# Inner norms: all squares added on VectorE, sums and spread inside running units, and a branch product moved ahead

## The chip, the core and the metric

The kernel runs on one core of one Trainium2 chip. The metric is the device time of one execution in microseconds (us). The engines are TensorE (PE, its weight loads PEld), VectorE (DVE), ScalarE (ACT), GpSimd (POOL) and SyncE (SP), whose queue issues most DMAs.

## The reference

One sequence of 512 tokens of width 1024 goes through two blocks. Cut to what matters:

```python
h = h + 0.5 * swiglu(rmsnorm(h, ffn1_norm), ...)           # "ffn1"
u = rmsnorm(h, mix_norm)                                   # "mix"
(fq, fk, fv, ff, dq, dk, dv, iq, ik, iw, mq, g) = jnp.split(u @ w_in, SPLIT_POINTS, axis=-1)
...                                                        # three attentions o_a, o_b, o_c
proj = jnp.einsum('bsnw,nwd->bsnd', branches, w_branch)    # the branches
h = h + jnp.sum(sigmoid(g) * proj, axis=2) @ w_out
h = h + 0.5 * swiglu(rmsnorm(h, ffn2_norm), ...)           # "ffn2"
# second block
z = rmsnorm_2(h, g_mix_2) @ w_in_2 + b_in_2                # "mix2"
h = h + y @ w_out_2                                        # y: a convolution and a pooling of z
h = h + swiglu_2(rmsnorm_2(h, g_ffn_2), ...)               # "ffn3"
return rmsnorm_2(h, g_final)                               # "final"
```

`rmsnorm` divides each token by the root of the mean of its squares and multiplies by a gain. All is float32.

## The kernel before

Everything is held transposed: channels on 128 partitions, the 512 tokens along the free axis, so the residual `h` is 8 chunks of 128x512. Weights come as units of 128x1024, `RING` = 4 of them in flight. For exactness each factor is split in a rounded high part and a low rest, and `products` (L498 on) makes three matmuls of one step: high x high, weight low x high, weight high x low. A unit of a projection (`project`) is 8 such steps, 24 matmuls. For a unit, SyncE's queue loads the raw weight once the unit four earlier is done, ScalarE casts it to its high part (`high`, L984; called through `after(u)`, which casts unit u + 2), GpSimd subtracts to get the low part (`low_part`, L435), and TensorE waits for `low_done`.

A norm works like this. The product before it ends in eight banks. `feed` on VectorE adds each bank to the residual (L1411) and, one chunk later, makes the low part of the input (L1361); `feed` on ScalarE makes the input's high part (L992) and the square of the chunk (L995) into `tiles[m]`. The norm's factor is applied only behind the products, so TensorE starts at once with the first two units, interleaved (`pair_start`). The squares are added up: tiles 0 to 4 by GpSimd (`add_squares`, L451), tiles 5 to 7 and the total by VectorE (`total_squares`, L1378). `sums` on TensorE (L573) sums over channels, ScalarE takes the root (`feed_root`, L1006), VectorE the reciprocal (L1368), `spread_factor` on TensorE (L581) spreads it over the partitions, and VectorE copies it to `token_factor` (L1401), where every consumer of the products waits for it. At the first norm, ffn1, VectorE adds all squares, and sums and spread stand inside the third and the fourth unit. At the inner norms (mix, ffn2, mix2, ffn3) `sums` stands behind `pair_start` and `spread_factor` right behind it, ahead of the third unit.

In the gated layers VectorE scales the gate and the up product (L1426, L1431), ScalarE applies Silu (L1107), VectorE multiplies (L1436), ScalarE casts the hidden chunk (L1112), VectorE makes its low part (L1441). In ScalarE's program order the cast of the fifth unit's weights stands behind the first hidden chunk's cast.

In the mix projections each head norm squares its output, GpSimd makes the squares' low part (L480) and TensorE sums them (L655).

The branches: for chunk m = 0 to 7 of the output there are three products `branch(m, n)` of four steps each (12 matmuls); three products use one and a half weight units. Products (0, 0) and (0, 1) read attention outputs that are split early, (0, 2) those of the memory attention, which ScalarE casts (L1240) and VectorE splits (L1650, `out_split`) last. GpSimd then alternates weight products with the scaling of the last gates (L486).

Engines run their own instruction lists in program order and meet only through semaphores, so the order written in the code is the order on the engine.

## Time and profile before

| | us |
|---|---|
| median of 3 runs | 1805.9 |
| lowest, highest | 1804.47, 1806.55 |
| the profiled execution | 1804.1 |
| its span, first to last instruction | 1802.3 |
| TensorE matmuls busy | 1769.3 |
| VectorE, ScalarE, GpSimd busy | 696.1, 698.4, 798.7 |
| TensorE's mean granted clock | 0.997 of full speed |

A row of the timeline gives the start and the duration of an instruction, or of a few equal ones in a row (x8), and in brackets how long its engine idled before it and what ended that. Matmuls overlap: one of 512 columns is shown with 0.39 us, but the next starts after some 0.23 us, so lost time is best read from starts.

### The profile page before, as it was taken

The numbers are of one execution on the slowest core, as the hardware profiler recorded it, in microseconds if no ns is written. First come the engines' busy times: TensorE is split into PE (matmuls) and PEld (weight loads), VectorE is DVE, ScalarE is ACT, GpSimd is POOL, SyncE is SP. The second block draws the span as 40 slices with busy tenths as digits, with TensorE's granted clock in tenths as the row PEclk, the third lists the DMA queues.
The fourth block names the chain that finished last, engine by engine and source line by source line (L and its number), as shares of the span: only waits on it lengthen the run. The fifth ranks groups of instructions, "written<-read, shape, count | busy, mean of one in ns | idle before, by whom it ended". The sixth has DMA issues, their size and how long they took to land.

```text
span 1802.3 us, 23345 instructions
## 1 busy us (share of the span) xinstructions
PE 1769.3 (98%) x8472; PEld 1435.3 (80%) x8472; DVE 696.1 (39%) x1141; ACT 698.4 (39%) x1120; POOL 798.7 (44%) x368
## 2 busy tenths in 40 slices
PE   9999999999999999999999999999999999999997
PEld 7888888877887777787878888888766788888886
DVE  5222230077867875235252222200775422222002
ACT  5322321164544477784342232211425432322212
POOL 2444444456565433334444444444533444444442
PEclk9999999999999999999999999999999999999998
DMA  5222322322333121112222233223251222232231
GB/s 177 100 93 94 103 95 93 127 84 79 106 116 110 63 70 45 48 48 93 94 93 94 93 96 102 93 93 104 89 141 61 91 93 93 98 100 93 95 103 70
DMA packets 50495, 168.23 MB, mean 93 GB/s; under 512 B 6264, under 2 KB 7032, under 8 KB 50304
## 3 DMA queue, kind: packets, MB, share of 16 engines
q1 hardware_dynamic: 47088, 161.34, 27.3%
q10 hardware_dynamic: 3344, 6.05, 1.1%
q8 instruction: 40, 0.66, 0.2%
q14 instruction: 23, 0.19, 0.0%
HBM read 161.84 MB, written 2.11 MB: 91 GB/s over the span
## 4 chain that ended last, share of the span: by engine, by line
PE 91%; DVE 5%; ACT 2%; DMA 1%; issue 1%; SPq 0%; POOL 0%; DVEq 0%; ACTq 0%
PE bank L502 25%; PE bank L504 25%; PE bank L503 25%; PE bank L716 8%; PE bank L761 2%; DVE input_low L1361 2%; PE bank L787 2%; PE bank L884 1%; PE bank L778 1%; DMA raw_weights<-weights 1%; DVE bank L1511 1%; DVE residual L1411 1%; PE bank L581 0%; PE bank L767 0%; ACT tile L1193 0%
## 5 line engine op out<-in xcount | busy, mean ns | idle before, releaser
L435 POOL TENSOR_TENSOR weights_low<-raw_weights,weights_high 128x1024 fp32r<-128x1024 f32 x292 | 707.8, 2426 | 941.4 <-ACT weights_high L984 919.4
L502 PE MATMUL bank<-input_high,weights_high 128*128 128x512 f32 x1424 | 557.9, 392 | 6.1 <-DVE input_low L1361 5.3
L503 PE MATMUL bank<-input_high,weights_low 128*128 128x512 f32 x1424 | 554.4, 389 | 0.0
L504 PE MATMUL bank<-input_low,weights_high 128*128 128x512 f32 x1424 | 554.3, 389 | 0.0
L984 ACT CAST weights_high<-raw_weights 128x1024 fp32r<-128x1024 f32 x294 | 307.0, 1047 | 307.3 <-DMA raw_weights<-weights 290.0
L502 PEld LDWEIGHTS bank<-input_high,weights_high 128*128 128x128 f32 x1424 | 267.3, 188 | 69.2 <-DVE input_low L1361 8.8
L504 PEld LDWEIGHTS bank<-input_low,weights_high 128*128 128x128 f32 x1424 | 267.3, 188 | 56.2
L503 PEld LDWEIGHTS bank<-input_high,weights_low 128*128 128x128 f32 x1424 | 267.4, 188 | 54.4 <-issue 0.2
L502 PE MATMUL bank<-hidden_high,weights_high 128*128 (+1 forms) x528 | 205.4, 389 | 0.0
L503 PE MATMUL bank<-hidden_high,weights_low 128*128 (+1 forms) x528 | 205.4, 389 | 0.0
L504 PE MATMUL bank<-hidden_low,weights_high 128*128 (+1 forms) x528 | 205.4, 389 | 0.0
L1431 DVE TENSOR_TENSOR tile<-bank,token_factor 128x512 f32<-128x512 f32 x66 | 45.6, 691 | 300.3 <-PE bank L504 300.3
L1112 ACT CAST hidden_high<-tile 128x512 f32 (+1 forms) x66 | 41.1, 622 | 303.4 <-DVE tile L1436 303.4
L1411 DVE SCALAR_TENSOR_TENSOR residual<-bank,residual 128x512 f32<-128x512 f32 x40 | 27.3, 684 | 259.1 <-PE bank L504 259.1
L503 PEld LDWEIGHTS bank<-hidden_high,weights_low 128*128 128x128 f32 x528 | 99.1, 188 | 20.7
L502 PEld LDWEIGHTS bank<-hidden_high,weights_high 128*128 128x128 f32 x528 | 99.1, 188 | 20.5
L504 PEld LDWEIGHTS bank<-hidden_low,weights_high 128*128 128x128 f32 x528 | 99.1, 188 | 20.5
L1107 ACT ACTIVATE tile<-tile 128x512 f32<-128x512 f32 x66 | 41.9, 634 | 181.1 <-DVE tile L1426 181.1
L1426 DVE TENSOR_TENSOR tile<-bank,token_factor 128x512 f32<-128x512 f32 x66 | 45.7, 692 | 137.1 <-PE bank L504 136.2
L716 PE MATMUL bank<-input_high,weights_high 128*128 128x512 f32 x192 | 78.1, 407 | 0.4 <-DVE tile L1459 0.4
L716 PE MATMUL bank<-input_high,weights_low 128*128 128x512 f32 x192 | 76.8, 400 | 0.0
L716 PE MATMUL bank<-input_low,weights_high 128*128 128x512 f32 x192 | 76.7, 399 | 0.0
(243 smaller groups left out, 1844.2 us busy)
## 6 DMA issues: line engine op xcount, KB each, us to landing
raw_weights<-weights SPq DMA_DIRECT2D x294, 512.0 KB, 3.4
out_t<-out_t SPq DMA_DIRECT2D x8, 256.0 KB, 2.1
residual<-x_t SPq DMA_DIRECT2D x6, 256.0 KB, 5.8
glu_stacked<-glu_padded ACTq DMA_DIRECT2D x24, 64.0 KB, 3.8
glu_stacked<-glu_padded SPq DMA_DIRECT2D x24, 64.0 KB, 3.7
mem_in<-mem_t ACTq DMA_DIRECT2D x1, 1024.0 KB, 4.9
tile<-forget_sums ACTq DMA_DIRECT2D x4, 256.0 KB, 3.6
raw_weights<-weights SPq DMA_DIRECT2D x3, 256.0 KB, 5.6
```

Of the source, the lines that this page charges most:

```text
L435: pool.tensor_tensor(wl[:, u % RING, :], raw[:, u % RING, :], wh[:, u % RING, :].bitcast(F32), ALU.subtract).then_inc(low_done, 1)
L502: pe.matmul(out, wh[:, u % RING, w], rh, start=start, stop=False)
L503: pe.matmul(out, wl[:, u % RING, w], rh, start=False, stop=False)
L504: return pe.matmul(out, wh[:, u % RING, w], rl, start=False, stop=stop)
L716: mm = pe.matmul(bank[g % 2][:, :], (wl if part == 1 else wh)[:, u % RING, w], (xl if part == 2 else xh)[:, k, :], start=(k == 0 and part ...
L761: mm = pe.matmul(score_banks[n % 3][:, cols], left, right[:, cols], start=True, stop=not (kind == "fox" and last))
L984: act.copy(wh[:, u % RING, :], raw[:, u % RING, :]).then_inc(high_done, 1)
L1107: act.activation(tiles[c][:, :], tiles[c][:, :], ACT.Silu).then_inc(sem(f"{name}_silu"), 1)
L1112: act.copy(hh[:, f, :].rearrange("p a n -> p (a n)"), tiles[2 + c][:, :]).then_inc(sem(f"{name}_high"), 1)
L1411: dve.scalar_tensor_tensor(out=h[:, m, :], in0=bank[m][:, :], scalar=share, in1=h[:, m, :], op0=ALU.mult, op1=ALU.add).then_inc(sem("resid ...
L1426: dve.tensor_tensor(tiles[c][:, :], bank[2 * c][:, :], rstd[:, :], ALU.mult).then_inc(sem(f"{name}_gate"), 1)
L1431: dve.tensor_tensor(tiles[2 + c][:, :], bank[2 * c + 1][:, :], rstd[:, :], ALU.mult).then_inc(sem(f"{name}_banks"), 1)
```

## The change

Six things are changed.

1. At the inner norms VectorE adds all eight squares in one row of seven additions, as at ffn1; GpSimd adds none, but for the final norm.
2. In ffn2 and ffn3 the sums stand inside the third unit, behind its fourth step, and the spread inside the fourth unit, behind its second step. In mix and mix2 the sums stand behind the first step of the third unit and the spread behind its fourth.
3. In ffn2 and ffn3 ScalarE casts the fourth unit's weights ahead of the root.
4. In mix VectorE's two small casts of the ones (L1581, L1582) stand ahead of the additions.
5. The branches of chunks 0 and 1 come in the order (0,0), (0,1), (1,0), (0,2), (1,1), (1,2). GpSimd makes the low part of weight U_BR+2 ahead of the last gate's scaling, but only once all twelve outputs are split.
6. The sigmoids of chunk m wait for the gates of that chunk, not for all 24.

```diff
@@ gpsimd
             low_parts(DVE_LOWS, U_IN + 2)
-            add_squares("mix")
@@
                 low_part(gate_unit(g) + 2)
+                if g == GATES - 1:
+                    pool.wait_ge(sem("out_split"), 12)
+                    low_part(U_BR + 2)
                 pool.wait_ge(sem("gates_out"), g + 1)
                 pool.tensor_tensor(gate_slot(g), gate_slot(g), rstd[:, :], ALU.mult)
-            low_parts(U_BR + 2, U_GU2 + 2)
-            add_squares("ffn2")
+            low_parts(U_BR + 3, U_GU2 + 2)
             low_parts(U_GU2 + 2, U_IN2 + 2)
-            add_squares("mix2")
             low_parts(U_IN2 + 2, U_GU3 + 2)
-            add_squares("ffn3")
@@ tensor, project
                     if k == behind:
                         inside()
+                    if then and k == behind + 3:
+                        then()
@@ tensor, gate_up
-                    spread_factor(feed)
-                    project(u0 + 2, bank[2][:, :], xh, xl, u0 + 3)
-                    project(u0 + 3, bank[3][:, :], xh, xl, u0 + 4)
+                    project(u0 + 2, bank[2][:, :], xh, xl, u0 + 3, inside=lambda: sums(feed), behind=3)
+                    project(u0 + 3, bank[3][:, :], xh, xl, u0 + 4, inside=lambda: spread_factor(feed), behind=1)
@@ tensor, mix (and the same in mix2)
                         if j == 2:
-                            spread_factor("mix")
+                            project(U_IN + j, proj[j % 3][:, 0:n], rh, rl, U_IN + j + 1, n, inside=lambda: sums("mix"),
+                                    behind=0, then=lambda: spread_factor("mix"))
@@ tensor, branches
-            for m in range(DK):
+            for m, n in ((0, 1), (1, 0), (0, 2), (1, 1), (1, 2)):
+                branch(m, n)
+            for m in range(2, DK):
                 for n in range(3):
-                    if m or n:
-                        branch(m, n)
+                    branch(m, n)
@@ scalar, gate_up
                         if c == 0 and i is None:
-                            feed_root(feed_name, bank[4])
                             if u0:
                                 after(u0 + 1)
+                            feed_root(feed_name, bank[4])
@@ scalar, sigmoids
+                act.wait_ge(sem("gates_scaled"), 2 * DK + m + 1)
@@ vector, total_squares
-                for i, m in enumerate((*range(POOL_SQUARES + 1, DK), 0)):
...
+                for m in range(1, DK):
+                    dve.wait_ge(sem("input_square"), fed(name, m))
...
                     dve.tensor_tensor(tiles[0][:, :], tiles[0][:, :], tiles[m][:, :], ALU.add
                                       ).then_inc(sem("squares_totalled"), 1)
@@ vector, mix
             feed("mix", "mix_norm", "g1", U_IN - 1, 0.5)
+            dve.tensor_copy(bd_r[:, :], bd[:, :]).then_inc(sem("ones_rounded"), 1)
+            dve.tensor_copy(ones_r[:, :], ones[:, :]).then_inc(sem("ones_rounded"), 1)
             factor("mix")
             dve.wait_ge(sem("sine_signed"), P // HD)
-            dve.tensor_copy(bd_r[:, :], bd[:, :]).then_inc(sem("ones_rounded"), 1)
-            dve.tensor_copy(ones_r[:, :], ones[:, :]).then_inc(sem("ones_rounded"), 1)
```

How this reads on the engines. TensorE's list at the norm of mix, before; L573 are the sums, L581 the spread:

```order
L503 MATMUL bank<-input_high,weights_low 128x512
L504 MATMUL bank<-input_low,weights_high 128x512
L573 MATMUL bank<-ones,tile_107 128x1 x4
L581 MATMUL bank<-identity,token_root 128x128 x4
L502 MATMUL bank<-input_high,weights_high 128x512
L503 MATMUL bank<-input_high,weights_low 128x512
L504 MATMUL bank<-input_low,weights_high 128x512
```

and now, where the rows ahead of L573 belong to the third unit's first step:

```order
L504 MATMUL bank<-input_low,weights_high 128x512
L573 MATMUL bank<-ones,tile_107 128x1 x4
L502 MATMUL bank<-input_high,weights_high 128x512
L503 MATMUL bank<-input_high,weights_low 128x512
L504 MATMUL bank<-input_low,weights_high 128x512
L502 MATMUL bank<-input_high,weights_high 128x512
L503 MATMUL bank<-input_high,weights_low 128x512
L504 MATMUL bank<-input_low,weights_high 128x512
L502 MATMUL bank<-input_high,weights_high 128x512
L503 MATMUL bank<-input_high,weights_low 128x512
L504 MATMUL bank<-input_low,weights_high 128x512
L581 MATMUL bank<-identity,token_root 128x128 x4
```

The sums moved behind three matmuls, the spread behind nine more. ScalarE's list at ffn2, from the end of the feed, before; L984 casts a unit's weights, L1006 is the root, L1107 Silu, L1112 the cast of a hidden chunk:

```order
L995 ACTIVATE tile_114<-residual 128x512
L984 CAST weights_high<-raw_weights 128x1024
L1006 ACT_TABLE_LOAD
L1006 ACTIVATE token_root<-bank,epsilons 128x4
L984 CAST weights_high<-raw_weights 128x1024
L1107 ACT_TABLE_LOAD
L1107 ACTIVATE tile_107<-tile_107 128x512
L1112 CAST hidden_high<-tile_109 128x512
L984 CAST weights_high<-raw_weights 128x1024
L1107 ACTIVATE tile_108<-tile_108 128x512
```

and now, with the lines shifted by four:

```order
L999 ACTIVATE tile_114<-residual 128x512
L988 CAST weights_high<-raw_weights 128x1024 x2
L1010 ACT_TABLE_LOAD
L1010 ACTIVATE token_root<-bank,epsilons 128x4
L1111 ACT_TABLE_LOAD
L1111 ACTIVATE tile_107<-tile_107 128x512
L1116 CAST hidden_high<-tile_109 128x512
L988 CAST weights_high<-raw_weights 128x1024
L1111 ACTIVATE tile_108<-tile_108 128x512
```

The cast of the fourth unit's weights moved ahead of the root; that of the fifth still stands behind the first hidden chunk. GpSimd's list at the last gates, with the semaphores waited for, before:

```order
L486 TENSOR_TENSOR gates_last<-gates_last,token_factor 128x512 [waits gates_out]
L435 TENSOR_TENSOR weights_low<-raw_weights,weights_high 128x1024 [waits high_done]
L486 TENSOR_TENSOR gates_last<-gates_last,token_factor 128x512 [waits gates_out]
L435 TENSOR_TENSOR weights_low<-raw_weights,weights_high 128x1024 [waits high_done]
L486 TENSOR_TENSOR gates_end<-gates_end,token_factor 128x512 [waits gates_out]
L435 TENSOR_TENSOR weights_low<-raw_weights,weights_high 128x1024 [waits high_done] x2
```

and now:

```order
L489 TENSOR_TENSOR gates_last<-gates_last,token_factor 128x512 [waits gates_out]
L435 TENSOR_TENSOR weights_low<-raw_weights,weights_high 128x1024 [waits high_done]
L435 TENSOR_TENSOR weights_low<-raw_weights,weights_high 128x1024 [waits high_done,out_split]
L489 TENSOR_TENSOR gates_end<-gates_end,token_factor 128x512 [waits gates_out]
L435 TENSOR_TENSOR weights_low<-raw_weights,weights_high 128x1024 [waits high_done]
L442 UNCONDITIONAL_BRANCH
```

One weight product moved ahead of the last gate's scaling, with a wait of its own for the split outputs.

## Rows read from the trace of the kernel before

**Rows 1.** The page's part 1: busy us of each engine, its share of the span, instructions

```profile
PE 1769.3 (98%) x8472; PEld 1435.3 (80%) x8472; DVE 696.1 (39%) x1141; ACT 698.4 (39%) x1120; POOL 798.7 (44%) x368
```

**Rows 2.** Waits of TensorE, whole span: who, for whom, us in total, times, longest

```profile
PE bank L502 <- DVE input_low L1361: 5.3, 11, 0.8
PE bank L502 <- DVE mem_out_low L1650: 3.5, 3, 1.8
PE bank L581 <- DVE token_root L1368: 3.3, 5, 0.7
```

**Rows 3.** Timeline, TensorE, second norm (ffn2): start us, us, engine, line, operation, shapes, [idle]

```profile
929.82 0.98 PE L573 MATMUL bank<-ones,tile 128*128 128x1 f32 x8
931.43 1.16 PE L581 MATMUL bank<-identity,token_root 128*128 128x128 f32 x8 [0.64 <-DVE token_root L1368]
932.34 0.48 PE L502 MATMUL bank<-input_high,weights_high 128*128 128x512 f32 x1
```

**Rows 4.** Timeline, TensorE, first norm (ffn1), where sums and spread lie inside units

```profile
24.67 0.95 PE L573 MATMUL bank<-ones,tile 128*128 128x1 f32 x8
25.48 0.48 PE L502 MATMUL bank<-input_high,weights_high 128*128 128x512 f32 x1
25.80 0.39 PE L503 MATMUL bank<-input_high,weights_low 128*128 128x512 f32 x1
...
27.61 1.05 PE L581 MATMUL bank<-identity,token_root 128*128 128x128 f32 x8
```

**Rows 5.** Groups and one line, VectorE, feed of ffn2; timeline of VectorE and GpSimd there

```profile
L1361 DVE SCALAR_TENSOR_TENSOR input_low<-residual,vectors,input_high 128x512 fp32r<-128x512 f32 x8 | 10.3, 1282 | 1.9 <-ACT input_high L992 1.8
...
L1361 DVE SCALAR_TENSOR_TENSOR input_low<-residual,vectors,input_high x8: 735/1181/2373, 912.0 to 924.8; 128x512 fp32r<-128x512 f32 x8
...
923.93 1.63 DVE L1361 SCALAR_TENSOR_TENSOR input_low<-residual,vectors,input_high 128x512 fp32r<-128x512 f32 x2
...
920.30 1.30 POOL L451 TENSOR_TENSOR tile<-tile,tile 128x512 f32<-128x512 f32 x1 [0.87 <-ACT tile L995]
```

**Rows 6.** Timeline, third add of squares on VectorE, and the weight product on GpSimd

```profile
926.92 2.76 DVE L1378 TENSOR_TENSOR tile<-tile,tile 128x512 f32<-128x512 f32 x1
...
926.38 2.76 POOL L435 TENSOR_TENSOR weights_low<-raw_weights,weights_high 128x1024 fp32r<-128x1024 f32 x1 [4.78 <-ACT weights_high L984]
```

**Rows 7.** Timeline, ffn2 behind the spread: ScalarE's cast, GpSimd's product, TensorE's fifth unit

```profile
936.29 1.05 ACT L984 CAST weights_high<-raw_weights 128x1024 fp32r<-128x1024 f32 x1
...
937.42 2.41 POOL L435 TENSOR_TENSOR weights_low<-raw_weights,weights_high 128x1024 fp32r<-128x1024 f32 x1 [2.92 <-ACT weights_high L984]
...
943.34 0.39 PE L502 MATMUL bank<-input_high,weights_high 128*128 128x512 f32 x1
```

**Rows 8.** Timeline, branches' third product: TensorE, then GpSimd, then VectorE

```profile
810.97 0.47 PE L502 MATMUL bank<-mem_out_high,weights_high 128*128 128x512 f32 x1 [1.02 <-DVE mem_out_low L1650]
...
812.58 0.50 PE L502 MATMUL bank<-mem_out_high,weights_high 128*128 128x512 f32 x1 [0.67 <-DVE mem_out_low L1650]
...
815.35 0.50 PE L502 MATMUL bank<-mem_out_high,weights_high 128*128 128x512 f32 x1 [1.81 <-DVE mem_out_low L1650]
...
807.88 2.40 POOL L435 TENSOR_TENSOR weights_low<-raw_weights,weights_high 128x1024 fp32r<-128x1024 f32 x1 [12.79 <-ACT weights_high L984]
810.23 1.75 POOL L486 TENSOR_TENSOR gates_end<-gates_end,token_factor 128x512 f32<-128x512 f32 x1
...
809.78 6.12 DVE L1650 TENSOR_TENSOR mem_out_low<-mem_q,mem_out_high 128x512 fp32r<-128x512 f32 x4 [2.04 <-ACT mem_out_high L1240]
```

**Rows 9.** Timeline, mix: sums and spread, the cast of the ones, the heads' first norm sum

```profile
381.58 0.95 PE L573 MATMUL bank<-ones,tile 128*128 128x1 f32 x8
383.17 1.05 PE L581 MATMUL bank<-identity,token_root 128*128 128x128 f32 x7 [0.64 <-DVE token_root L1368]
...
385.09 1.63 DVE L1581 CAST ones_by_head_rounded<-ones_by_head 128x128 fp32r<-128x128 f32 x1
...
391.13 0.47 PE L655 MATMUL bank<-square_high,ones_by_head_rounded 128*128 128x512 f32 x1 [0.94 <-POOL square_low L480]
```

More of the change, by code:

```diff
@@ L301, in squares @@
         def squares(name):
-            return INPUTS.index(name) * (POOL_SQUARES - 1) + (DK - 1) * (name != "mix")
+            return (DK - 1) + (POOL_SQUARES - 1) * (name == "final")
         def totalled(name):
-            return DK - 1 + INPUTS.index(name) * (DK - POOL_SQUARES)
+            return (INPUTS.index(name) + 1) * (DK - 1) - (POOL_SQUARES - 1) * (name == "final")
         def nth(name):
@@ L504, in products, with project @@
                 return pe.matmul(out, wh[:, u % RING, w], rl, start=False, stop=stop)
-            def project(u, out, rh, rl, low_at, n=S, inside=None, behind=None, low=low_done):
+            def project(u, out, rh, rl, low_at, n=S, inside=None, behind=None, low=low_done, then=None):
                 pe.wait_ge(low, low_at)
@@ L562, in pair_start @@
                             mm.then_inc(unit_done, 1)
-                if name != "ffn1":
-                    sums(name)
             def sums(name):
@@ L635, in stepped @@
                             pe.wait_ge(sem("mem_low"), DK)
+                        rh, rl = (mem_h, mem_l) if n == MEM else (xh, xl)
                         if j == 2:
-                            spread_factor("mix")
-                        rh, rl = (mem_h, mem_l) if n == MEM else (xh, xl)
-                        project(U_IN + j, proj[j % 3][:, 0:n], rh, rl, U_IN + j + 1, n)
+                            project(U_IN + j, proj[j % 3][:, 0:n], rh, rl, U_IN + j + 1, n, inside=lambda: sums("mix"),
+                                    behind=0, then=lambda: spread_factor("mix"))
+                        else:
+                            project(U_IN + j, proj[j % 3][:, 0:n], rh, rl, U_IN + j + 1, n)
                     else:
@@ L679, in stepped @@
                     if j == MEM_STEP + 11:
-                        pe.wait_ge(sem("squares_added"), squares("mix") + DK - 1)
+                        pe.wait_ge(sem("squares_added"), squares("mem"))
                         for b in range(MEM // P):
@@ L831, in branch @@
                                   rh[:, o + k, :], rl[:, o + k, :], k == 0, k == BK - 1)
-                    if b % DK == DK - 1:
+                    if (b % DK == DK - 1 and b != 2 * DK - 1) or (m, n, k) == (0, 2, BK - 1):
                         mm.then_inc(unit_done, 1)
@@ L932, in _ @@
                 if j == 2:
-                    spread_factor("mix2")
-                project(U_IN2 + j, proj[j % 3][:, :], xh, xl, U_IN2 + j + 1)
+                    project(U_IN2 + j, proj[j % 3][:, :], xh, xl, U_IN2 + j + 1, inside=lambda: sums("mix2"),
+                            behind=0, then=lambda: spread_factor("mix2"))
+                else:
+                    project(U_IN2 + j, proj[j % 3][:, :], xh, xl, U_IN2 + j + 1)
                 if j in CONV_AFTER:
@@ L1370, in total_squares @@
             def total_squares(name):
-                for i, m in enumerate((*range(POOL_SQUARES + 1, DK), 0)):
-                    if m:
-                        dve.wait_ge(sem("input_square"), fed(name, m))
-                    else:
-                        dve.wait_ge(sem("squares_added"), squares(name))
-                    total = tiles[POOL_SQUARES] if m else tiles[0]
-                    dve.tensor_tensor(total[:, :], tiles[POOL_SQUARES][:, :], tiles[m][:, :], ALU.add
-                                      ).then_inc(sem("squares_totalled"), 1)
-                    dve.wait_ge(sem("squares_totalled"), totalled(name) - (DK - POOL_SQUARES) + i + 1)
-            def total_first_squares():
                 for m in range(1, DK):
-                    dve.wait_ge(sem("input_square"), fed("ffn1", m))
-                    if m == 5:
+                    dve.wait_ge(sem("input_square"), fed(name, m))
+                    if name == "ffn1" and m == 5:
                         dve.wait_ge(high_done, 4)
@@ L1390, in total_first_squares, with total_last_squares @@
                                       ).then_inc(sem("squares_totalled"), 1)
-                    dve.wait_ge(sem("squares_totalled"), m)
+                    dve.wait_ge(sem("squares_totalled"), totalled(name) - (DK - 1) + m)
+            def total_last_squares():
+                for i, m in enumerate((*range(POOL_SQUARES + 1, DK), 0)):
+                    if m:
+                        dve.wait_ge(sem("input_square"), fed("final", m))
+                    else:
+                        dve.wait_ge(sem("squares_added"), squares("final"))
+                    total = tiles[POOL_SQUARES] if m else tiles[0]
+                    dve.tensor_tensor(total[:, :], tiles[POOL_SQUARES][:, :], tiles[m][:, :], ALU.add
+                                      ).then_inc(sem("squares_totalled"), 1)
+                    dve.wait_ge(sem("squares_totalled"), totalled("final") - (DK - POOL_SQUARES) + i + 1)
             def factor(name):
-                if name == "ffn1":
-                    total_first_squares()
-                else:
-                    total_squares(name)
+                total_squares(name)
                 inverse(name)
@@ L1809, in _ @@
             feed("final", None, "g3", UNITS - 1, 1.0, parts=False)
-            total_squares("final")
+            total_last_squares()
             inverse("final")
```

7 lines of the change are left out of this document (3 added, 4 removed).

## The prediction

> **What bounds the kernel now.** I read the page's busy table first: TensorE's matmul pipe is busy 1769.3 of 1802.3 us and GpSimd 798.7 [rows 1]. So only idle time of TensorE, or matmuls slower than their neighbours, can be won. The table of TensorE's waits, read next, names what there is [rows 2]: 5.3 us in 11 waits for VectorE's low halves of the input (L1361), 3.3 us for the reciprocal of the inner norms (L1368) and 3.5 us for the low halves of the memory attention's output (L1650). The change aims at these three. A busy share hides that matmuls overlap, so I count from start to start: a full product is 0.226 us (eight of them lie between 25.80 and 27.61), and the first one after a break takes 0.32 [rows 4].
>
> **One inner norm, before.** At ffn2 the eight sums of squares start at 929.82, the spread of the factor at 931.43 after 0.64 us of idling, the next product at 932.34 [rows 3]: 2.52 us without a product, 2.61 with the slow first one. I call the start of the sums P and count each site from its own P (mix 381.58, the others lie alike). The same two pieces of work inside running units cost 0.81 + 0.09 us for the sums and the same for the spread, 1.80 together, as the first norm shows, which already has this form [rows 4]. That is 0.8 us a site to be won, 3.2 over four, if nothing else becomes late.
>
> **What VectorE gains in the feed and pays in the adds.** The eight low halves at ffn2 take 8 x 1.282 = 10.26 us, though the shortest takes 0.735. The first one waits for a weight product (2.37); the other seven at 0.735 would make 7.52 in all, so 2.7 us are lost [rows 5]. The lost time lies beside GpSimd's adds of squares, 1.30 us each [rows 5]. Without these adds VectorE ends the last low at 922.86 instead of 925.56 (929.82 - 4.26), which is P - 6.97, and the waits of the paired first two units go (1.4 us at ffn2), so their end moves to about P - 1.4.
> But VectorE now adds seven pairs, not three. Free, one takes 0.725 from start to start, seven 5.1. One that meets a weight product of GpSimd takes 2.76 where that product took 2.76 from 926.38 [rows 6]: 2.07 us extra. The trace shows this of a third add and never of a row of seven, so the bound below is no extra (the rival on this is below), the upper bound one such meeting for each product that falls into the row. I take the latter, as the only row shows it. In ffn2 and ffn3 there are two products, since ScalarE's cast of the fourth unit's weights now stands ahead of the root: 5.1 + 4.1 = 9.2 us. In mix2 one, 7.15; in mix one and two small casts (0.2 each) moved ahead, 7.6.
>
> The Trainium skill (SBUF — State Buffer, Who interferes with whom) says that a VectorE instruction with two SBUF inputs and a GpSimd one that reads SBUF exclude each other for the whole instruction, whichever came first. By it the adds pay as I have summed; without it the sum is that of the second case below. The row of the third add agrees, no row shows how the two take turns over seven adds.
>
> **ffn2 and ffn3.** Sums start at P - 6.97 + 9.2 = P + 2.25 (TensorE is there at P - 1.4 + 12 products, 2.7, = P + 1.3, and waits 0.9). Then 0.9 of sums, 18 products (4.08), spread at P + 7.25. Now what is behind the spread: factor copied, gate product, Silu, up product, cast of the first hidden chunk, and only then ScalarE's cast of the fifth unit's weights at 936.29, and GpSimd's product 937.42 to 939.83 [rows 7]. From spread to that end it is 939.83 - 931.43 = 8.40 us. TensorE before came to the fifth unit at 943.34 [rows 7], 3.5 us after it was ready: this cover hid the chain. Now only six of eight steps of the fourth unit (0.9 + 4.08) follow the spread; 3.4 us are missing. Fifth unit after: P + 7.25 + 8.40 + 0.1 = P + 15.75; before: 943.34 - 929.82 = P + 13.52. **Loss 2.2 us, twice.** The paired units' waits drop out of this, as the chain hangs on VectorE; ffn3's longer ones (it has three) don't matter.
>
> **mix2.** Sums at P - 6.97 + 7.15 + 0.05 = P + 0.25; with 0.9, nine products, spread 0.9 and twelve products (6.56) the fourth unit starts at P + 6.8. Before P + 2.61 + 24 products = P + 8.05. **Gain 1.25 us.** The factor reaches VectorE 1.6 us later; VectorE there runs ahead of TensorE later on, so I cost that at nothing; if that cover is gone it costs up to 1.6.
>
> **mix.** Sums at P + 0.7. The first norm sum of the heads (L655) waits for a chain that begins at the spread: before from 383.17 to 391.13, of which the cast of the ones held 1.63 us plus its gap, 1.7 [rows 9]; the cast is now ahead. So 6.26 from the spread, which is 0.9 + 2.04 behind the sums: P + 9.9 against P + 9.55. The gain in front turns into a longer wait here (0.94 before). **Loss 0.3 us, of which I keep 0.2**, since VectorE's next steps start a little earlier; between +1 and -1.2 (sums not waiting).
>
> **The branches.** Before, three products waited, at 810.97, 812.58 and 815.35, 1.02, 0.67 and 1.81 us idle [rows 8], with slow restarts 4.2. VectorE's four low halves took 6.12 us [rows 8] instead of some 2.9: the first lay behind GpSimd's product to 810.28, the second behind the gate multiply, the third behind the next product. Now branch 0 of the second chunk stands in the gap (12 products, 2.73), and GpSimd waits for the twelfth split with the weight U_BR+2. Queued behind that wait on GpSimd are the last gate and U_BR+3. TensorE would be there at 809.8 (the first wait, 810.97, less its length), but needs the low half of U_BR+1, ready at 810.28 [rows 8], starts 810.4 and is done at 813.2. VectorE's first low half still ends half a microsecond behind that product, 810.8; the other three at about 0.6 from start to start are done at 812.7, so (0,2) runs through, 12 products to 815.95. Before, six products followed the last restart at 815.35, to 816.8, and (1,0) took 2.73 more, to 819.55: 3.6 us. U_BR+2 is low 2.4 us after the splits, about 815.1, just ahead of its use at 815.95. Later VectorE's merges meet GpSimd's products, now 3.6 us closer to TensorE, which costs me 0.5. **Gain 3.1 us**, bounds 1.5 and 4.2.
>
> **Sum.** +2.2 + 2.2 - 1.25 + 0.2 - 3.1 = +0.25 us. The profiled run took 1804.1 (span 1802.3 and 1.8 around it), 1.8 below the median 1805.9; as a shift it gives 1806.1, and I say **1806.0**. About 0.2% (3.6 us) is what a measurement here can tell from no change.
>
> **The cases.**
> 1. As summed, 1806.0 (its own range 1803 to 1809). Chance 0.66.
> 2. The seven adds don't meet the products as one by one as I assume (the products wait, or one add only is held). Then the sums wait nowhere: 0.9 and 1.9 us less at ffn2 and ffn3, 0.75 at mix2, 1.4 at mix: 1806.0 - 4.95 = 1801.0. For it: two adds ran free beside the start of a product at 926.38. Against: the third was held for all of it. 0.15.
> 3. The fifth unit is not late, since the chain behind the spread is shorter than 8.40 or starts earlier. Then 3.5 less twice: 1799. Against: each link follows the last within 0.1 to 0.3 us, none waited for TensorE. 0.07.
> 4. Slower: in the branches the held product pushes GpSimd's queue, VectorE's additions of the merges (two SBUF inputs) each meet a product (2.07 each, 4.1 a chunk) and ScalarE's casts, which stand behind the merges, come late. Before, the tightest weights were low 1.6 us ahead of use, so a chunk hit twice costs 2.5; at the three tightest places (U_BR+5, +8, +11) 7.5, less the 0.5 counted: two of three give 1806 + 4.5 = 1810.5. It decides once both additions of a chunk are hit. 0.12.
>
> Cases 1 and 2 make 0.81, and the range reaches over both: **1800.5 to 1809.5**. Faster by over 0.2% (under 1802.3) are cases 2 and 3: 0.22. Slower (above 1809.5) is case 4: 0.12. Same: 0.66.
>
> **What would show it.** In the trace after: the lows of the feed all near 0.74 but the first; no wait of TensorE in the paired units except a short one at ffn3; seven adds of 0.69 with two of some 2.8 in them; the sums starting 2.2 us after the old P in ffn2 and ffn3, 0.7 in mix, 0.25 in mix2, each behind a wait for L1382; at the fifth unit of ffn2 and ffn3 a wait of 3.4 us for GpSimd's low weights, which the table of waits before doesn't have at all; L655 in mix waiting over 2 us; the waits for the memory attention's low halves gone but for one of 0.6 for a weight. If the wait at the fifth unit isn't there, my largest term is wrong; if the adds run in 5.1 us, the second.

## The result, and the profile of the changed kernel

The changed kernel took 1815.29 us (median of 7 executions, 1809.75 to 1818.66), the kernel before 1804.84 in the same session (7 executions, 1803.86 to 1807.46): a ratio of 1.0049, 95% interval 1.0039 to 1.0059. The forecast was 1806.0, with a range that ended at 1809.5. The change makes the kernel slower by 0.5%, and the range missed it by almost 6 us. The profiled execution took 1816.41 us, span 1814.6.

The waits of TensorE in the trace after, in the columns of [rows 2]:

```profile
PE bank L502 <- POOL weights_low L435: 6.9, 4, 3.1
PE bank L573 <- DVE tile L1382: 4.4, 4, 1.9
PE bank L656 <- POOL square_low L479: 4.2, 3, 2.0
...
PE bank L502 <- DVE tile L1523: 2.1, 1, 2.1
...
PE bank L581 <- DVE token_root L1373: 0.7, 1, 0.7
PE bank L502 <- DVE input_low L1366: 0.5, 1, 0.5
```

The three waits of [rows 2] that the change aims at are gone or nearly so: 0.5 us are left of 5.3 for the input's low halves, 0.7 of 3.3 for the reciprocal (the final norm's, which the change leaves alone), and the waits for the memory attention's low halves aren't in the table any more. In their place stand the two that the prediction had named, the fifth unit of ffn2 and ffn3 (3.12 and 3.11 us) and the sums that wait for VectorE's adds. So far the forecast holds. One long wait stands here that the prediction doesn't have: 2.15 us for VectorE (L1523) in mix, where TensorE waited 0.65 before. But the page's busy table, the line of [rows 1], has this:

```profile
PE 1781.1 (98%) x8472; PEld 1445.7 (80%) x8472; DVE 709.4 (39%) x1157; ACT 696.7 (38%) x1120; POOL 778.2 (43%) x352
```

TensorE does the same 8472 instructions and is busy 11.8 us longer than before. No wait does that; its instructions themselves became slower. The view of windows shows where. Its columns are the stretch in us, its length, the busy time and instruction count of each engine, then the granted clock of TensorE (PEclk, 1.00 is 2.4 GHz and 0.50 is 1.2 GHz). Four stretches of before, then the same of after:

```profile
380.00:480.00 100.00, 94.09 (x448) 76.54 (x447) 80.11 (x73) 53.48 (x87) 60.67 (x35) 1.00 0.28 91
810.00:830.00 20.00, 16.54 (x70) 13.09 (x71) 13.79 (x16) 11.23 (x19) 10.01 (x5) 1.00 0.24 79
925.00:955.00 30.00, 29.36 (x138) 24.43 (x138) 12.10 (x16) 11.96 (x15) 14.76 (x6) 1.00 0.27 88
1430.00:1455.00 25.00, 24.36 (x116) 20.30 (x115) 12.03 (x16) 11.59 (x15) 11.98 (x5) 1.00 0.26 85
```

```profile
380.00:480.00 100.00, 92.61 (x418) 74.58 (x417) 76.88 (x70) 53.38 (x87) 59.78 (x34) 0.95 0.26 83
810.00:830.00 20.00, 19.62 (x91) 16.07 (x90) 13.37 (x18) 13.60 (x22) 10.84 (x5) 1.00 0.24 79
925.00:955.00 30.00, 25.97 (x108) 20.75 (x107) 16.09 (x15) 8.39 (x11) 12.92 (x5) 0.89 0.21 70
1430.00:1455.00 25.00, 23.12 (x96) 18.88 (x95) 14.95 (x18) 9.04 (x12) 5.63 (x2) 0.86 0.25 81
```

In the branches (810 to 830) TensorE does 91 instructions where it did 70: the waits of [rows 8] are gone. In mix and around the two inner feed-forward norms the granted clock is 0.95, 0.89 and 0.86 of full, where it was 1.00. Narrow windows find the places; these are three of the seven:

```profile
392.30:395.70 3.40, 3.40 (x9) 2.63 (x9) 1.84 (x1) 3.35 (x7) 2.90 (x2) 0.50 0.00 0
...
948.70:952.10 3.40, 3.40 (x10) 2.62 (x9) 1.99 (x1) 1.17 (x2) 3.40 (x2) 0.51 0.02 5
1443.60:1450.40 6.80, 6.80 (x20) 5.54 (x20) 0.18 (x1) 1.55 (x2) 0.00 (x0) 0.50 0.00 0
```

The others begin at 423.0, 474.2, 935.0 and 1460.7. The first of these stretches in the trace before:

```profile
392.30:395.70 3.40, 3.40 (x16) 2.81 (x16) 2.06 (x1) 3.35 (x7) 2.70 (x2) 1.00 0.13 52
```

At the full clock 3.4 us hold 16 instructions of TensorE, here 9 or 10. Together it is 27.3 us at 1.2 instead of 2.4 GHz, of which half, 13.65 us, is lost. The Trainium skill (TensorE: Matmul & The Clock Gate, Terms) prices time at the low level by one half in the same way; the instruction counts agree. In the profile of before there is none ahead of the last 12 us. (It is one of the best executions of that kernel: its mean clock is 0.997, those of its 52 executions in the experiments' sessions go down to 0.994, and 0.003 of 1802 us is 5.4 us. So the kernel before, too, has such stretches in some executions; no trace shows where.)

The timeline of TensorE at ffn2's sums and at the fifth unit shows what precedes the falls (start, duration, [idle before]):

```profile
932.77 1.05 PE L573 MATMUL bank<-ones,tile 128*128 128x1 f32 x8 [0.92 <-DVE tile L1382]
...
934.93 0.56 PE L504 MATMUL bank<-input_low,weights_high 128*128 128x512 f32 x1
935.28 0.63 PE L502 MATMUL bank<-input_high,weights_high 128*128 128x512 f32 x1
935.71 0.63 PE L503 MATMUL bank<-input_high,weights_low 128*128 128x512 f32 x1
...
947.77 0.50 PE L502 MATMUL bank<-input_high,weights_high 128*128 128x512 f32 x1 [3.12 <-POOL weights_low L435]
948.11 0.39 PE L503 MATMUL bank<-input_high,weights_low 128*128 128x512 f32 x1
948.34 0.40 PE L504 MATMUL bank<-input_low,weights_high 128*128 128x512 f32 x1
948.57 0.55 PE L502 MATMUL bank<-input_high,weights_high 128*128 128x512 f32 x1
948.92 0.63 PE L503 MATMUL bank<-input_high,weights_low 128*128 128x512 f32 x1
```

Behind the restart a product starts every 0.23 us up to 948.57, and from 948.92 on every 0.43 us. All seven stretches lie like that, within 2.3 us of the end of a wait: behind 382.1 to 391.4 (waits of 1.00 and 1.97 us), 422.8 (2.15), 474.0 (1.77), 932.8 (0.92), 947.8 (3.12), 1443.1 (1.88) and 1459.7 (3.11). Six of these waits are new or longer than before. The one up to 474.0 isn't: before, TensorE waits 1.79 us at the same place, up to 470.4, and the clock stays up.

The place of each stage's first TensorE instruction in the two traces gives the price by stage:

| stage | difference, us | half clock in it, us lost | left | predicted |
|---|---|---|---|---|
| mix | +3.7 | 5.1 | -1.4 | +0.2 |
| branches | -3.2 | 0 | -3.2 | -3.1 |
| ffn2 | +5.6 | 3.4 | +2.2 | +2.2 |
| mix2 | -1.1 | 0 | -1.1 | -1.25 |
| ffn3 | +6.9 | 5.1 | +1.8 | +2.2 |
| end | +0.4 | | +0.4 | 0 |
| sum | +12.3 | 13.65 | -1.3 | +0.25 |

The row of mix has in it 0.2 us by which the changed kernel was later already at the end of ffn1.

### The profile page after: what moved, and what is told of

Read it like the earlier page. It is cut to its first block, busy times and chain, and to the rows that moved or that the text cites. A ratio compares the mean times of both kernels' runs of the same rounds, so it can differ in the third digit from the quotient of the medians.

```text
span 1814.6 us, 23348 instructions
## 1 busy us (share of the span) xinstructions
PE 1781.1 (98%) x8472; PEld 1445.7 (80%) x8472; DVE 709.4 (39%) x1157; ACT 696.7 (38%) x1120; POOL 778.2 (43%) x352
## 4 chain that ended last, share of the span: by engine, by line
PE 63%; issue 21%; POOL 10%; DVE 3%; ACT 2%; DMA 1%; POOLq 0%; SPq 0%; DVEq 0%; ACTq 0%
PE bank L502 16%; PE bank L503 16%; PE bank L504 16%; POOL weights_low L435 10%; PE bank L717 8%; PE bank L762 2%; PE bank L788 2%; PE bank L779 1%; DMA raw_weights<-weights 1%; DVE bank L1513 1%; ACT input_high L996 1%; DVE tile L1382 0%; ACT tile L999 0%; PE bank L768 0%; ACT tile L1197 0%
## 5 line engine op out<-in xcount | busy, mean ns | idle before, releaser
L1413 DVE SCALAR_TENSOR_TENSOR residual<-bank,residual 128x512 f32<-128x512 f32 x40 | 27.3, 682 | 259.1 <-PE bank L504 259.1
```

## The experiments

**Theory A:** the loss is TensorE's clock, which falls behind waits that the change makes longer or new. **Theory B** (the rival): the clock falls by itself or by chance, and the two have nothing to do with each other; the loss would stay when the waits go. For each kernel the span of every execution times its mean granted clock tells what it would take at 2.4 GHz throughout; the rest is what the clock cost. This is a split, not a law: a fall inside a wait costs less, and slow products shorten the waits behind them. Means over all executions, in us:

| kernel | median | ratio to before, 95% | at full clock | by the clock |
|---|---|---|---|---|
| before (three sessions) | 1805.1 to 1806.2 | 1 | 1795.8 | 8.0 |
| changed | 1815.3 | 1.0049 (1.0039 to 1.0059) | 1795.2 | 17.3 |
| branches_alone | 1801.7 | 0.9977 (0.9967 to 0.9986) | 1793.1 | 7.0 |
| norms_alone | 1816.7 | 1.0051 (1.0033 to 1.0069) | 1798.7 | 15.9 |
| early_cast | 1803.4 | 0.9984 (0.9975 to 0.9994) | 1789.2 | 12.2 |
| hold_10 | 1814.9 | 1.0048 (1.0031 to 1.0065) | 1801.4 | 11.8 |
| hold_7 | 1808.1 | 1.0013 (1.0004 to 1.0023) | 1798.2 | 8.1 |
| mix_restored | 1799.1 | 0.9965 (0.9953 to 0.9978) | 1789.9 | 7.8 |
| late_sums | 1800.5 | 0.9973 (0.9962 to 0.9984) | 1786.8 | 12.2 |
| combined | 1796.8 | 0.9951 (0.9934 to 0.9967) | 1788.5 | 6.3 |
| root_first | 1811.2 | 1.0033 (1.0022 to 1.0043) | 1794.9 | 14.5 |

Some 5 to 7 us of the last column are in every kernel: the clock is low through the final norm's waits at the very end.

The rows come from different sessions. In that of branches_alone, norms_alone, early_cast and hold_10 the kernel before stood at 1795.4 and 8.9, in that of mix_restored, late_sums, combined and root_first at 1796.0 and 7.7, in that of hold_7 at 1796.0 and 7.6. The mean clock is known to 0.001, which is 1.8 us of one execution. So differences of less than 1 us between two rows show nothing.

**branches_alone.** The kernel before with the branch part of the change alone (the order of the products, GpSimd's weight ahead of the last gate, the later semaphore counts, the sigmoids' waits):

```diff
-            for m in range(DK):
-                for n in range(3):
-                    if m or n:
-                        branch(m, n)
+            for m, n in ((0, 1), (1, 0), (0, 2), (1, 1), (1, 2)):
+                branch(m, n)
...
+                if g == GATES - 1:
+                    pool.wait_ge(sem("out_split"), 12)
+                    low_part(U_BR + 2)
```

> The kernel before with the branch part of the change alone (order of the products, GpSimd holding U_BR+2, sigmoids by chunk). Theory A (the loss is TensorE's clock: after its waits at the norms products run at half clock for some 3.4 us, eight such stretches in the profile after, 27 us at half clock, 13.7 us lost; without them the change would be 1.3 us faster): the branch part has no new long wait, so a mean granted clock of 0.997 as before and 3 to 4 us less than before, 1801. Theory B (the clock falls by itself in this build or session, whatever waits there are): mean clock 0.99 as in the changed kernel and a time some 8 us above before.

Measured: 1801.73 (10 executions), no half-clock stretch in its profile before the end. From the end of mix to the first product of the merged branches its trace is 3.2 us shorter than before, as in the changed kernel. Against the kernel before of its own session it gains 4.4 us, 2.3 at full clock and 1.9 by the clock; the waits of [rows 8] are gone in it. This part is worth keeping.

**norms_alone.** The changed kernel with the branch part undone, that is the other half alone.

> The changed kernel with the branch part undone: the norm part alone. Theory A: it carries all of the new waits, so all of the loss: after plus the 3.1 to 3.6 us that the branches gave, about 1816 to 1819, mean clock 0.988 to 0.992, half-clock stretches behind the waits for squares and at the fifth unit of ffn2 and ffn3. Theory B: no relation to the waits.

Measured: 1816.71 (4 executions). The whole loss is in the norms; the branch part hides some of it. Its profile has seven stretches at half clock: five at the same waits as in the changed kernel's, one at 383.4 behind the sums of mix, and one at 820.3 beside the old wait of 1.81 us of [rows 8].

**early_cast.** The changed kernel, with ScalarE's cast of the fifth unit's weights right behind the root in ffn2 and ffn3 instead of behind the first hidden chunk:

```diff
-                        if u0 or i is not None:
+                        if (u0 and c == 0) or i is not None:
                             after(u0 + 2 * c, i)
                         if c == 0 and i is None:
                             if u0:
                                 after(u0 + 1)
                             feed_root(feed_name, bank[4])
+                            if u0:
+                                after(u0 + 2)
```

> The changed kernel with one line moved: in ffn2 and ffn3 ScalarE casts the fifth unit's weights right behind the root and not behind the first hidden chunk. Theory A: the two waits of 3.3 us at the fifth unit go, and with them the half-clock stretches that follow them (1.7 us each): 10 us less than the changed kernel, about 1805; mean clock up by 0.002. Theory B: 6.6 us less, as many half-clock stretches as in the changed kernel. If the chain behind the spread is bounded by something else than this cast, the wait stays near 3 us.

Measured: 1803.38 (10 executions). The cast stands at 932.50, GpSimd's product at 933.62, and the fifth unit starts with no wait:

```profile
932.50 1.04 ACT L988 CAST weights_high<-raw_weights 128x1024 fp32r<-128x1024 f32 x1
...
933.62 2.38 POOL L435 TENSOR_TENSOR weights_low<-raw_weights,weights_high 128x1024 fp32r<-128x1024 f32 x1 [5.16 <-ACT weights_high L988]
```

At full clock it is 6.0 us below the changed kernel, which is the two waits of 3.1; another 5.1 came back by the clock, where theory B expects none. So the two waits had cost nearly twice their length. Left are the stretches at 391.6, 473.5 and, behind the 1.94 us wait of ffn3's sums, 6.8 us from 1436.0.

**hold_10 and hold_7.** The opposite test: the kernel before, with nothing changed but ten or seven chained copies on ScalarE ahead of the cast of the fifth unit's weights, so that TensorE waits there as it does in the changed kernel, or for a shorter time:

```diff
+                        if u0 and c and i is None:
+                            for k in range(10):
+                                act.copy(tiles[8][:, :], tiles[7][:, :]).then_inc(sem("held"), 1)
+                                act.wait_ge(sem("held"), 10 * (u0 == U_GU3) + k + 1)
```

> The kernel before, with ten copies on ScalarE (tile 7 to tile 8, some 0.68 us each, nobody reads them) ahead of the cast of the fifth unit's weights in ffn2 and ffn3: a wait of some 3.3 us there and nothing else of the change. Theory A: the wait is paid more than once: 2 x 3.3 us and 2 x 1.7 us of half clock, 10 us above before, 1815, and products spaced 0.43 us behind each wait. Theory B: 6.6 us, clock 0.997.

> The kernel before with seven chained ScalarE copies instead of ten ahead of the cast of the fifth unit's weights in ffn2 and ffn3: each copy and its gap was worth some 0.6 us, so TensorE should wait about 1.0 us there instead of 2.83. The idle time itself costs 2 x 1.0: about 1807 by both theories if a wait of this length has no clock behind it; if the clock falls there as behind the wait of 2.83 us (3.41 us at half clock), 1.7 us more for each fall.

The waits were 2.83 us in hold_10 and 0.90 in hold_7, twice each. hold_10: 1814.91 (4 executions), 8.8 us above before for 5.7 us of idle time. At the first of the waits TensorE's windows read

```profile
949.80:953.20 3.40, 3.40 (x10) 2.61 (x9) 1.99 (x1) 1.07 (x2) 3.40 (x2) 0.51 0.02 5
1459.70:1466.50 6.80, 6.77 (x30) 5.61 (x31) 3.22 (x3) 1.85 (x3) 5.60 (x2) 1.00 0.01 4
```

so the clock fell behind the one and not behind the other. hold_7: 1808.07 (10 executions), 3.0 us above before for 1.8 us of idle time. Behind its new waits the clock stays up:

```profile
948.80:952.00 3.20, 3.20 (x14) 2.62 (x15) 2.83 (x1) 0.31 (x1) 2.30 (x1) 1.00 0.49 169
1456.50:1459.70 3.20, 3.20 (x14) 2.67 (x15) 2.82 (x1) 0.33 (x1) 2.28 (x1) 1.00 0.51 164
```

Against the kernel before of their own sessions the short waits cost 0.5 us by the clock (8.1 against 7.6), less than can be told, the long ones 2.9 us (11.8 against 8.9). So waits alone, in a kernel otherwise unchanged, bring the clock down, and not each wait does. In both kernels the profile also shows falls at old waits (472.0 and 813.3; 406.7 and 816.3), of which the profile of before has none: two of the three stretches of hold_10 are not behind the new waits.

**hold_10_again and changed_again.** Both once more, unchanged, for a second trace of each.

> The kernel before with the ten chained copies once more, for a second trace: in the first the clock fell at 472.0 and 813.3 (behind waits that the kernel before has too) and at 949.8 (the new wait), and not behind the new wait at 1459.7. Theory A with a fixed answer of the clock to each wait: the same three. If the answer varies from execution to execution, other waits of over a microsecond are followed by it, and the time stays within 1812 to 1817.

> The changed kernel once more, for a second trace of it: does the granted clock fall at the same places? Theory A: again behind the waits of mix (382 to 392, 423, 474), behind ffn2's sums or its fifth unit and behind ffn3's, six to eight stretches, 1813 to 1818. Theory B: elsewhere, away from the waits.

hold_10_again has one stretch, at 947.6, behind the same new wait as the first time, and none at 472 or 813: 1814.91 again (2 executions). changed_again: 1815.14 (3 executions), stretches at 384.5, 408.4, 944.3 (6.8 us), 1442.6 and 1456.3. The first two lie behind waits of 1.06 and 1.85 us; in the first trace the one was 1.00 us long with no fall behind it, the other only 0.51. Those at 423 and 474 are not there: the wait for L1523 is 0.2 us long instead of 2.15, and the one of 1.78 us up to 473.4 has no fall. So a fall also moves the waits behind it. The falls keep to the waits, but which wait gets one changes from execution to execution. It fits with this that the changed kernel scatters over 8.9 us and the kernel before over 4.8 at most.

Over the 13 profiles (before, changed, the eleven of the experiments) there are 35 half-clock stretches ahead of the final norm. Each begins inside a wait of TensorE or at most 2.3 us behind the end of one; none lies in the hundreds of microseconds between. All waits of over 0.3 us, with 2.3 us behind each, are 3% of these traces. Of the 53 waits of over 1.5 us, 30 had a fall beside them, of the 167 shorter ones (over 0.3) 7. A fall that comes wherever it likes, as theory B has it, would not keep to that 3%. But theory A is too narrow as it stands: falls come behind old waits too, where these are long. And of the seven short waits four are the one of 0.9 to 1.1 us ahead of a norm's sums, which are themselves eight products of one column each (the other three are in the branches, in the row of waits of [rows 8]). Whether those small products help the clock to fall no experiment here tells apart from the wait.

**mix_restored.** early_cast with the mix norm as in the kernel before: GpSimd adds four squares, sums and spread between units.

```diff
             low_parts(DVE_LOWS, U_IN + 2)
+            add_squares("mix")
...
-                            project(U_IN + j, proj[j % 3][:, 0:n], rh, rl, U_IN + j + 1, n, inside=lambda: sums("mix"),
-                                    behind=0, then=lambda: spread_factor("mix"))
+                            spread_factor("mix")
```

> The early cast once more, with the mix norm as in the kernel before (GpSimd adds four squares, sums and spread between the units). The early cast had two half-clock stretches in mix (391.6 and 473.5) and its head sums ended 2.5 us later than in the branches alone: 3.4 of clock less 0.9 won in front. Theory A (the clock falls behind new or longer waits of TensorE): with the old short waits there the two stretches go, about 1800.9, granted clock about 0.995. Theory B (the clock falls by itself): as many stretches as with the early cast, only the 0.9 comes back on: about 1804.3.

Measured: 1799.10 (6 executions), 4.3 us below early_cast, of which 1.0 is the sessions' (by the kernel before of each). Set against the kernel before of its own session, each is 6.1 or 6.2 us better at full clock, so the table shows no gain of the change in mix by itself; by the clock the old arrangement is 3.3 us better (0.1 above before, early_cast 3.4). Its profile has none of the stretches between 380 and 480, though the waits of 1.87 and 1.77 us are in it as in the kernel before. One stretch was left, at 1434.6. Theory A had said 1800.9, theory B 1804.3.

**late_sums.** early_cast with the sums of ffn2 and ffn3 four steps later and the spread one:

```diff
-                    project(u0 + 2, bank[2][:, :], xh, xl, u0 + 3, inside=lambda: sums(feed), behind=3)
-                    project(u0 + 3, bank[3][:, :], xh, xl, u0 + 4, inside=lambda: spread_factor(feed), behind=1)
+                    project(u0 + 2, bank[2][:, :], xh, xl, u0 + 3, inside=lambda: sums(feed), behind=DK - 1)
+                    project(u0 + 3, bank[3][:, :], xh, xl, u0 + 4, inside=lambda: spread_factor(feed), behind=2)
```

> The early cast with the sums of ffn2 and ffn3 four steps later, behind the third unit's last step, and the spread one step later. The waits for the seven adds (0.80 and 1.94 us) are covered by 12 products. Theory A: with ffn3's wait the 6.83 us at half clock behind it go too (3.4 us of loss): 1803.4 - 2.7 - 3.4 = 1797.3. Theory B: only the idle time goes, the stretch comes at that place or another: 1800.7.

Measured: 1800.49 (8 executions). The waits for the adds in ffn2 and ffn3 are gone, a wait of 0.5 at the fifth unit is left, and both stages run at full clock:

```profile
934.40:950.00 15.60, 15.10 (x75) 12.43 (x74) 8.38 (x11) 7.86 (x11) 7.03 (x3) 1.00 0.30 100
1437.00:1452.00 15.00, 14.51 (x73) 11.96 (x72) 8.38 (x11) 6.98 (x10) 6.15 (x3) 1.00 0.25 81
```

At full clock 2.4 us below early_cast (2.7 expected), but on average nothing came back by the clock (12.2 both): the profile has its three stretches all in mix, at 392.2, 422.9 and 474.1. The 1797.3 of theory A was missed by 3.2 us, and the 1800.7 of theory B met to 0.2: on the total this experiment speaks for B. In the one profile ffn3's fall is gone with its wait, as theory A says; that the average clock didn't rise with it (the falls in mix must have become more) is not explained, since only one execution of each session has a trace.

**combined.** The branch part, mix as before, late sums and the early cast in ffn2 and ffn3, and mix2's sums three steps later:

```diff
-                            behind=0, then=lambda: spread_factor("mix2"))
+                            behind=3, then=lambda: spread_factor("mix2"))
```

> The branch part, mix as before, ffn2 and ffn3 with VectorE's adds, late sums and the early cast, mix2's sums three steps later. From the two kernels beside it: 1803.4 - 2.5 - 6.1 - 0.6 (mix2's wait) = 1794.2 by theory A, with a granted clock of 0.996 or more and no half-clock stretch but the last; by theory B about 1798 with several.

Measured: 1796.75 (4 executions, 1795.55 to 1797.26), ratio 0.9951, which beats both kernels, the changed one by some 18 us, and branches_alone as well. No half-clock stretch but the last. The same four windows as above read

```profile
380.00:480.00 100.00, 94.11 (x448) 76.48 (x447) 80.09 (x73) 53.38 (x87) 60.61 (x35) 1.00 0.27 91
810.00:830.00 20.00, 19.84 (x87) 16.44 (x88) 13.24 (x17) 12.95 (x22) 8.54 (x5) 1.00 0.30 106
925.00:955.00 30.00, 29.50 (x139) 24.37 (x138) 14.17 (x18) 9.92 (x13) 13.03 (x6) 1.00 0.27 92
1430.00:1455.00 25.00, 24.50 (x116) 20.20 (x115) 11.87 (x18) 9.14 (x13) 9.98 (x4) 1.00 0.26 96
```

It is 2.5 us above theory A's 1794.2 and 1.3 below theory B's 1798; that no half-clock stretch is in its profile, and that it has the smallest loss by the clock of all (6.3 us), is what A said. The step in mix2 won nothing: a wait of 0.8 us for VectorE at 1295.0 came instead, and the stage is as long as in mix_restored, 141.1 and 141.0 us.

**root_first.** The changed kernel with the cast of the fourth unit's weights behind the root again, so that only one GpSimd product can meet the seven adds:

```diff
+                            feed_root(feed_name, bank[4])
                             if u0:
                                 after(u0 + 1)
-                            feed_root(feed_name, bank[4])
```

> The changed kernel with ScalarE's cast of the fourth unit's weights behind the root again, as before, so that only one GpSimd weight product can fall into the row of seven adds. By the rule that one add is held for each product met (2.07 us), the seven adds of ffn2 take 5.1 + 2.1 = 7.2 us instead of 9.2 and the sums' wait for them there goes; if the adds share the port in another way, they stay at 9.2 or drop to 5.1. The fourth unit then waits for its low weights by about 1.5 us, so the time says little: 1812 to 1818.

Measured: 1811.22 (8 executions), 0.8 us below the expected range. The sums' wait in ffn2 is gone, and the fourth unit waits 0.91 us for its low weights (1.5 expected). The seven adds of the changed kernel, then those of root_first, each with GpSimd beside them:

```profile
923.52 9.20 DVE L1382 TENSOR_TENSOR tile<-tile,tile 128x512 f32<-128x512 f32 x7
...
924.36 5.63 POOL L435 TENSOR_TENSOR weights_low<-raw_weights,weights_high 128x1024 fp32r<-128x1024 f32 x2 [9.75 <-ACT weights_high L988]
```

```profile
922.47 7.11 DVE L1382 TENSOR_TENSOR tile<-tile,tile 128x512 f32<-128x512 f32 x7
...
923.30 2.82 POOL L435 TENSOR_TENSOR weights_low<-raw_weights,weights_high 128x1024 fp32r<-128x1024 f32 x1 [9.76 <-ACT weights_high L988]
```

9.20 us with two products, 7.11 with one: the second costs 2.09 (2.07 predicted), the first 2.0 over the 5.1 of seven free adds. Within the 7.11 us six adds take 0.68 or 0.69 us and one 2.76, as in [rows 6]. The trace of the changed kernel says the same by itself: its seven adds take 7.14 and 7.11 us in mix and mix2, with one product each, and 9.20 in ffn2 and in ffn3, with two. The Trainium skill (SBUF — State Buffer, Who interferes with whom) says that a VectorE instruction with two inputs in SBUF contends with a GpSimd one that reads SBUF. The rows agree, and they have the price: one add is held for each product.

## Why the prediction was right in its steps and wrong in its sum

**What failed: the sum, which priced every wait at its own length.** Its terms came out within 0.4 us, but for that of mix; TensorE's clock it put at nothing, without a reason. That "only idle time of TensorE, or matmuls slower than their neighbours, can be won" says its first part, but the second half was never carried on to "or lost": the granted clock, which the page prints, isn't mentioned in it. At full clock the changed kernel takes 1795.2 us against 1795.8 before, -0.6 where +0.25 was forecast, a difference that the table can't tell from none. The other 9.3 us are the clock. Five waits that the prediction itself lists (0.9 and 1.9 for the sums, 3.4 twice at the fifth unit, "over 2 us" in mix) were followed by a fall, at 1.7 us for each 3.4 us at half speed. No rival had it either: the slower case, 1810.5, rested on the merges of the branches which didn't happen; it lay nearer to the 1815.29 for a wrong reason.

A sign was to be seen. In the profile of before, TensorE waits 3.1 us for the final norm's sums at 1790.1, and the windows ahead of it and behind it read

```profile
1780.00:1790.00 10.00, 7.01 (x31) 5.46 (x30) 6.13 (x9) 5.34 (x8) 5.18 (x4) 1.00 0.00 0
1791.00:1801.00 10.00, 2.54 (x11) 2.19 (x10) 5.53 (x9) 0.26 (x1) 0.00 (x0) 0.50 0.52 194
```

The only wait in it as long as the two forecast for the fifth unit is the only one with the half clock behind it. TensorE does little else behind it, so it was a hint and not a proof, and at the end of the kernel it costs little.

**The feed.** Right. The lows take 0.735 to 0.74 us but for the one behind a weight product (2.39); the last ends at 923.60. Seven adds at 9.20, forecast 9.2.

**ffn2 and ffn3, +2.2 each.** Right in size and cause. The forecast for ffn2's sums is P + 2.25, here 932.6 with TensorE 0.6 us later at the stage's start; measured 932.77 behind a wait of 0.92 (0.9 forecast). The fifth unit waited 3.12 (3.4 forecast) for the low weights, behind the chain of [rows 7]. It starts at 947.77; the forecast's P + 15.75 would be 946.1, and the 1.7 us between are the fall at 935.0, which delays the spread and all behind it. Less the clock, the stages cost +2.2 and +1.8. early_cast shows that the waits hang on the place of ScalarE's cast: with it moved, 6.0 us are back at full clock.

**mix2, -1.25.** Right: -1.1, its sums behind a wait of 0.63.

**mix, +0.2.** The first norm sum of the heads stands where it was forecast, 0.2 us later than before (391.35 against [rows 9]), though nearly all of that was there ahead of the stage; it stands behind 1.97 us of waiting ("over 2 us"). The stage as a whole came out at -1.4 beside the clock, in the second trace of the changed kernel at -0.5. That the waits behind 400 us get shorter while the products are slow may explain a part; the rest is open. By mix_restored against early_cast, each against its own session, the change of mix is worth nothing that can be told at full clock, and costs 3.3 us by the clock.

**The branches, -3.1.** Right: -3.2. The products of (0,2) start at 816.88 with no wait, TensorE waits once on the way there, 0.38 us at 814.0 for GpSimd's low weights, and the four low halves, 6.12 us in [rows 8], take 2.85. The merges did not become late, so the slower case fell: one wait of 0.24 at 836.3 is all.

**Cases 2 and 3** fell too: the adds meet the products as counted, in the changed kernel and in root_first, and the fifth unit was late.

## What to carry to other kernels

A new wait of TensorE costs its length, and, if it is long, often the clock behind it too: in this kernel a wait of 3 us cost between 4 and 6 (hold_10: 8.8 us for two of 2.8; early_cast: 11.1 us back for two of 3.1), while waits of 0.9 us cost little beyond themselves. So several short waits can be better than one long wait of the same sum: the change turned eleven waits of up to 0.8 us, four of 0.64 and three in the branches into a few long ones, and it broke even at full clock but lost 9 us. Before forecasting, list the new waits with their lengths, look in the profile of before at what the granted clock did behind each of its own, and at the mean clock of its other executions, and put a term for it in the sum; where a step is moved off the critical path, ask first which chain behind it (here ScalarE's cast) can start earlier, since that removed the loss without giving up the move.

## What the hardware showed that was not expected

The clock falls in mid-kernel, in a TensorE that is 98% busy: behind waits of 0.9 to 3.1 us, to 0.50 of full, for 3.4 or 6.8 us, with products 0.43 us apart instead of 0.23. The Trainium skill (TensorE: Matmul & The Clock Gate, Wait — 56ns, not 53.3ns?) gives 426.7 ns for 512 columns at the low level; the rows show 0.43 us.

It is not the same from one execution to the next: the same kernel had falls at 472.0, 813.3 and 949.8 in one trace and at 947.6 alone in another. What decides it beside the length of the wait stays open; no experiment here was made to tell that apart.

What GpSimd costs a row of VectorE's two-input adds is simple to count: each weight product that falls into the row holds one add, 2.8 us instead of 0.69, and makes the row 2.0 to 2.1 us longer, the first product as the second.
